# Splitting a weight tile earlier in the attention: ahead of the next pair's masks and of the probability copy

## The reference, cut to what matters

```python
for i in range(DEPTH):                       # DEPTH = 4
    x = layer_norm(ALPHA * x + 0.5 * swiglu(x, ffn1_w13[i], ffn1_w2[i]), ...)
    # i = 0, 3: dsa_mixer; i = 1: fox_mixer; i = 2: mla_mixer
    x = layer_norm(ALPHA * x + y, ...)
    x = layer_norm(ALPHA * x + 0.5 * swiglu(x, ffn2_w13[i], ffn2_w2[i]), ...)
...
s = einsum('bqhd,bkhd->bhqk', q, k) * scale            # 16 heads
p = softmax(where(mask, s, -inf), axis=-1)
o = einsum('bhqk,bkhd->bqhd', p, v)
return o @ w_out
```

## Time and profile before

| | us |
|---|---|
| median of three runs | 2810.51 (2810.32 to 2813.01) |
| the profiled execution's own time | 2807.97 |
| its span, first to last instruction | 2806.2 |
| PE busy in the span | 2595.4 (92%) |
| DVE busy | 1527.7 (54%) |
| ACT busy | 1176.9 (42%) |
| mean granted TensorE clock | 0.948 of 2.4 GHz |

### The profile page before, as it was taken

The page is one execution under the profiler, slowest core; times in us unless marked ns, Lnnn a source line. Parts: engine busy times, 40 slices in busy tenths (PEclk is TensorE's granted clock), DMA queues, the critical chain, the costliest instruction groups (busy, mean ns, idle before and its releaser), DMA issues. The chain is left out here.

```text
span 2806.2 us, 32770 instructions
## 1 busy us (share of the span) xinstructions
PE 2595.4 (92%) x13229; PEld 2159.0 (77%) x13229; DVE 1527.7 (54%) x2248; ACT 1176.9 (42%) x1478; POOL 362.8 (13%) x465
## 2 busy tenths in 40 slices
PE   8998999999999999997899999989999874599898
PEld 6886878888887788886778888868788653498797
DVE  5555654464544555545564555555665647644555
ACT  4543454444444444443554444434444442133443
POOL 0001210000001000001310000012593014400000
PEclk9997999999999999998999999979999876699999
DMA  7553346555543565552345656533355310054454
GB/s 235 185 172 112 122 135 193 183 177 184 165 135 100 171 191 173 187 185 97 106 136 185 192 168 195 169 105 121 120 189 186 106 60 1 3 164 165 149 182 142
DMA packets 314968, 417.05 MB, mean 149 GB/s; under 512 B 18762, under 2 KB 273091, under 8 KB 314819
## 3 DMA queue, kind: packets, MB, share of 16 engines
q1 hardware_dynamic: 314818, 414.96, 46.1%
HBM read 413.87 MB, written 1.05 MB: 148 GB/s over the span
## 5 line engine op out<-in xcount | busy, mean ns | idle before, releaser
L416 DVE TENSOR_TENSOR wlo<-raw,whi 128x2048 fp32r<-128x2048 f32 (+3 forms) x402 | 913.8, 2280 | 689.2 <-ACT whi L408 688.9
L408 ACT ACTIVATE whi<-raw 128x2048 fp32r<-128x2048 f32 (+3 forms) x402 | 747.1, 1866 | 451.4 <-DMA raw<-in_ffn_w_dram 392.7
L528 PE MATMUL ps<-whi,xh 128*128 128x512 f32 (+4 forms) x2056 | 792.2, 385 | 30.3 <-DVE wlo L416 16.8
L529 PE MATMUL ps<-wlo,xh 128*128 128x512 f32 (+4 forms) x2056 | 778.0, 378 | 0.0
L530 PE MATMUL ps<-whi,xl 128*128 128x512 f32 (+4 forms) x2056 | 777.6, 378 | 0.0
L528 PEld LDWEIGHTS ps<-whi,xh 128*128 128x128 f32 x2056 | 397.7, 193 | 115.5 <-issue 30.4
L530 PEld LDWEIGHTS ps<-whi,xl 128*128 128x128 f32 x2056 | 397.0, 193 | 69.8
L529 PEld LDWEIGHTS ps<-wlo,xh 128*128 128x128 f32 x2056 | 398.5, 194 | 64.6
L528 PE MATMUL ps<-whi,oh 128*128 128x512 f32 x960 | 386.7, 403 | 5.9 <-DVE ol L1564 2.8
L530 PE MATMUL ps<-whi,ol 128*128 128x512 f32 x960 | 375.1, 391 | 0.0
L529 PE MATMUL ps<-wlo,oh 128*128 128x512 f32 x960 | 374.2, 390 | 0.0
(11 more groups left out here) (292 smaller groups left out, 2442.3 us busy)
## 6 DMA issues: line engine op xcount, KB each, us to landing
raw<-in_ffn_w_dram SPq DMA_DIRECT2D x352, 512.0 KB, 4.8
raw<-in_ffn_w_dram SPq DMA_DIRECT2D x88, 1024.0 KB, 4.9
raw<-in_w_ff_dram SPq DMA_DIRECT2D x32, 1024.0 KB, 5.2
raw<-in_w_out_dram SPq DMA_DIRECT2D x20, 1024.0 KB, 5.0
raw<-in_w_in_dram SPq DMA_DIRECT2D x20, 1024.0 KB, 5.1
raw<-in_dsa_w_in_dram SPq DMA_DIRECT2D x32, 512.0 KB, 4.4
raw<-in_dsa_w_in_dram SPq DMA_DIRECT2D x12, 1024.0 KB, 5.1
raw<-in_fox_w_in_dram SPq DMA_DIRECT2D x16, 512.0 KB, 4.4
```

Source lines behind the costliest of these rows:

```text
L408: act.activation(hi(u)[:, 0:w], raw[:, (slot[u] + 1) % SLOTS, 0:w], ACT.Copy).then_inc(sem("hi_ready"), 1)
L416: dve.tensor_tensor(lo(u)[:, 0:w], raw[:, (slot[u] + 1) % SLOTS, 0:w], hi(u)[:, 0:w].bitcast(F32), ALU.subtract).then_inc(sem("lo_ready"), 1)
L528: pe.matmul(o, ah, bh, start=start, stop=False, skip_group_check=True)
L529: pe.matmul(o, ah, bl, start=False, stop=False, skip_group_check=True)
```

## The change

In the loop over pairs ACT splits the high parts ahead of its copy of the turned probabilities, not behind it. DVE splits the low parts right behind the copy of q and k, ahead of the two `front` calls for the next pair and of its own copy of the probabilities. Nothing is added or removed, and the lists of PE and SP and the work of POOL are the same.

```diff
@@ ACT, the loop over pairs @@
                         if mla and q + 1 < NG:
                             latents(q + 1, 1 + i % 2)
+                        split_hi(act, attn_ahead(st, i))
                         turned_p(i)
-                        split_hi(act, attn_ahead(st, i))
                         if i + 1 < NP:
                             exps(2 * i + 2)
                             exps(2 * i + 3)
@@ DVE, the loop over pairs @@
                         for n in turns_at(st, i):
                             if mla or n % 2 == 0:
                                 turned_qk(n)
+                        split_lo(dve, attn_ahead(st, i))
                         if i + 1 < NP:
                             front(2 * i + 2)
                             front(2 * i + 3)
                         turned_p(i)
-                        split_lo(dve, attn_ahead(st, i))
```

## The result

The changed kernel takes 2841.77 us (median of 4 runs, 2835.93 to 2848.86), the kernel before 2810.85 in the same session: a ratio of 1.011, with a 95% interval of 1.0086 to 1.0133. It is slower by 31 us. The prediction said 2839, within 2823 to 2853. The profiled execution took 2841.87 us.

A forecast was written before the change was run, and what follows sets the result against it. PE was taken to bound the kernel, busy for 92% of the span. 2807.97 + 11.6 (dsa) + 0.2 (fox) + 7.0 (mla) + 3.0 (col) = 2829.8, with the clock 2837.3, about 2839 as median; range 2823 to 2853.

The forecast's parts named there:

- The start of the low parts: Second pair of dsa: ACT's copy from 302.34, first high part ends 304.75, DVE's low parts run 304.8 to 309.3.
- Second, fourth and sixth pair of dsa: PE's values wait 2.1 us at the second and fourth pair, 2.4 at the sixth; 5.8 net a stage.
- the step on the sixth pair: Dsa's sixth pair: values 2.4 us late, the seventh pair's 0.80 us wait for POOL absorbed, net 1.6.
- First, third and fifth pair of dsa: PE's narrow projection covers low parts and fronts: cost 0, or 0.5 us a pair if the cover were short.
- Fox: Fox attention: larger score matmuls just cover the 9.1 us chain; 0.2 us for the stage, bounds 0 and 1.5.
- Mla: Mla attention: fifth pair net 3.1 us, third 1.8, second and fourth 0.5, sixth to eighth 1.6; sum 7.0, bounds 3 and 10.
- Col: Col's third pair: values 4.3 us late, some lent by later POOL waits; 3.0 us taken, bounds 1 and 5.
- The clock: Lower PE clock behind about half the new dsa and mla waits: five stretches, 7.5 us, bounds 0 and 15.
- Hidden anyway: Rival for the whole kernel: the moves stay hidden, no change, about 2811 us; chance 0.09.
- Faster: Rival: earlier high parts remove waits for wlo in mla and POOL in dsa and col, 11.6 us; about 2799; chance 0.04.
- the three slower cases: Whole kernel: stalls, clock up, 2820 to 2831 (0.20); middle, 2831 to 2850 (0.53); clock falls nearly each, 2850 to 2862 (0.14).
- the forecast: Whole kernel: stalls plus some lower clock stretches, 2831 to 2850 us; chance 0.53.

The follow-up runs named there:

- e2: Only DVE's low parts moved ahead of the fronts and pT, ACT's list as before, against the kernel before: 3006.02 us, ratio 1.0708.
- e7: The change only at the first, third, fifth and seventh pairs of dsa, fox and col, against the kernel before: 2819.88 us, ratio 1.003.
- e6: The change in fox and col alone, old order elsewhere, against the kernel before: 2811.06 us, ratio 1.0011.
- e5: The change in the mla attention alone, old order elsewhere, against the kernel before: 2820.91 us, ratio 1.0039.
- e4: The change in the two dsa attentions alone, old order elsewhere, against the kernel before: 2821.98 us, ratio 1.0049.
- the repeated run: The changed kernel run once more, nothing altered, with more runs: 2834.31 us, ratio 1.0097 to the kernel before.
- e3: The changed kernel with high parts also ahead of ACT's copies of q and k and of the mla projection: 2811.4 us, ratio 1.0011 to before.
- e8: High parts ahead of ACT's copy of q and k, DVE's list as before, against the kernel before: 2804.42 us, ratio 0.9981.
- e11: Against e8, in col alone DVE's pT moved between the two fronts: 2801.39 us, ratio 0.9968 to the kernel before.
- e10: Against the changed kernel, DVE's pT moved right behind the low parts, ahead of both fronts: 2824.64 us, ratio 1.005 to the kernel before.
- e1: Only ACT's high parts moved ahead of its copy of the probabilities, DVE's list as before, against the kernel before: 2806.2 us, ratio 0.9993.
- e9: Against the changed kernel, DVE's low parts moved behind the two fronts, still ahead of pT: 2851.83 us, ratio 1.0146 to the kernel before.

## Why the prediction was right

**The start of the low parts.** The chain (ACT's copy of q and k, one high part, then both low parts) gave DVE's low parts a start 2.46 us behind the start of that copy, at 304.8 for 302.34. Measured: 307.41 - 304.97 = 2.44 us, and a duration of 4.50 us, as computed. The absolute times are 2.6 us later because the index stage ahead of this loop ran 3 us longer, at a lower clock.

**Second, fourth and sixth pair of dsa.** 2.1, 2.1 and 2.4 us predicted; 2.02, 2.02 and 2.53 measured, and again in the second stage (2.02, 2.02, 2.54). The 0.80 us for POOL was absorbed as the step on the sixth pair said, and 0.41 behind it that the prediction didn't count. So the stalls were 5.4 us a stage net, for 5.8 predicted. e2 shows the same arithmetic from the other end: 6.4 expected, 6.32 measured.

**First, third and fifth pair of dsa.** 0 predicted, and the changed kernel has no wait there: DVE's `pT` itself waits for PE, 0.36 us at the third pair and 1.02 at the fifth. e7 adds a condition that the prediction lacks: this cover holds only while the pairs between are in the new order as well.

**Fox.** 0.2 predicted, one wait of 0.3 us over the loop; e6 gives 0.3.

**Mla.** 7.0 predicted; PE is idle for 7.8 us more over the loop (14.90 for 7.06). That the sum is near is partly luck, for both sides of it were too small. The waits for `pT` rose by 12.2 us, from 2.0 to 14.2: the third pair waits 2.5 us more for 1.8 taken, the fifth 5.8 more for 5.3 (its two low parts took 4.94 us for 4.50), the other pairs 3.9 for 2.1. Against that went not only the 2.25 for `wlo` but the smaller waits named above as well, 4.7 us together, so `wlo` was not the only gain. The loop's other 3.4 us are clock. In e5 the same loop is 12.0 us longer (73.70 for 61.67), of which 7.6 idle and 4.5 busy, so the 10.3 to 11.4 us that e5 puts on mla have some 4 of clock in them.

**Col.** 3.0 predicted with a wait of 4.3 + 0.94 at the third pair; the wait is 4.90. Yet the profiles show col as quicker, 1.1 us from the first to the eighth `pT`. The windows over just that stretch, before and after:

```profile
2236.20:2294.93 58.73, 44.41 (x270) 34.31 (x269) 34.23 (x126) 27.78 (x86) 15.60 (x28) 0.73 0.17 55
```

```profile
2271.94:2329.53 57.59, 37.93 (x264) 29.21 (x263) 31.51 (x125) 25.93 (x83) 15.30 (x28) 0.87 0.16 55
```

In the profiled execution of before, PE's work in col ran at 0.73 and was busy for 6.5 us more (270 matmuls in its record, 264 in the other). e5, with col in the old order too, took 58.8 us for the stretch at 0.73, as before. But e4, also in the old order, took 55.6 at 0.86; e6, with col in the new one, took 57.6 at 0.87, as the changed kernel. So col costs 2.0 us (57.6 - 55.6) at a like clock, and a comparison of two single profiles had hidden it. PE is idle for 5.3 us more over the stretch than before (19.66 for 14.32) and for 3.4 more than in e4 (16.27). In the medians of e6 it can't be told from nothing.

**The clock.** 7.5 us predicted, as five lower stretches behind new waits. PE's busy time in the three loops that got new waits of 2 us is that term: 4.3 us more in the first dsa, 3.4 in mla and 1.4 in the second dsa (69.39 for 68.04), 9.1 in all, and 8.8 in the repeated run. So the term was right in place and near in size. Over the five loops together PE is idle for 24.0 us more, for 21.8 predicted. Yet the 31 us are not simply the sum of these two, since the clock moved in other places as well: the profiled execution was busy for 6.5 us less in col, in spite of the new wait there, for 1.5 less in fox and for 10.4 more outside the loops, where the index stage ahead of the first dsa loop was 3.0 us longer and the forget stage 6.3. These nearly cancel (+2.4 us), and that they do is luck; in the repeated run they come to -4.2 us (4.6 - 8.8). Of the six waits in dsa four were followed by 0.76 and two by 1.00. The Trainium skill, TensorE: Matmul & The Clock Gate, section What's actually happening, holds the lower clock for the default and activity for what releases it. The rows at 0.76 agree; those at 1.00 behind waits of the same 2.02 and 2.54 us show that a wait of that size doesn't always lead to the lower clock.

**The rivals.** "Hidden anyway" failed for the reason given, a slack of 1.3 us; e3 shows what it would have taken: high parts ahead of ACT's copies. "Faster" failed by the same place: the waits for `wlo` and POOL it counted on did go in dsa and mla, 3.9 us, and some 7 with the smaller ones beside them, against 30.4 more for `pT` (37.3 - 6.9). Of the three slower cases the forecast held.

What stays open: why the clock differs between executions with the same waits, and so whether the 2841.77 or the 2834.31 us is nearer to what the change costs. What is shown for both is 22 to 23 us of idle time of PE; no run held the clock fixed.

## What to carry to other kernels

An engine that is busy for half of the span is no free place in its list: what counts is the slack between one copy and the instruction that waits for it (here 1.3 us), and every wait that a moved step has on a third engine (here 2.2 us for ACT) is handed on to all that stands behind it. Move the producer first and alone, see that the consumer starts without idle time ahead of it, and keep the consumer behind the copy that the bounding engine waits for; that order (e8, with col's copy between the fronts in e11) was 0.32% faster, where the change that moved both was 1.1% slower. When two profiles are compared, take stages with unchanged code and the clock of each window as well, or a stage that lost 2 us reads as one that gained 1. Where both profiles have the same instructions, set PE's idle time against its busy time: the first changed by 22.4 and 23.0 us in two runs of one kernel, the second by 11.5 and 4.6.

## What the runs showed of the hardware

A wait of PE of 2.02 us was followed by a granted clock of 0.76 over seven microseconds at 314.10, 341.10 and 1978.70, and by 1.00 at 1953.20, in one execution. The longest waits in the repeated run (3.85 and 6.24 us, in mla) were followed by 0.58 and 0.64, in the first run by 0.76 and 0.73. Stages with the same instructions and no new wait moved by 3 to 6 us between executions (forget 46.90 and 53.16 us, at 0.96 and 0.84, with PE busy throughout in both and no wait in them), and one kernel's runs spread over 13 to 18 us (2835.93 to 2848.86, 2831.26 to 2849.68). From the norm's `xn` row to the first `pT` of fox, 13 of the 14 profiles took one of three times: 47.7 us at a clock of 0.96 (before, the repeated run, e4, e5, e6), 50.8 at 0.90 (e3, e8, e10) or 54.0 at 0.84 (the changed kernel, e1, e7, e9, e11); e2 took 60.4 at 0.86.
